# Moving the Gelu loads to ScalarE's queue, cutting the gate loads finer, and one exponential two units later

## What is computed

```
h = x + (sigmoid(ga) * (HGRN2(xn) @ W_a) + sigmoid(gb) * (FoX(xn) @ W_b)) @ W_out
h = h + PEER(RMSNorm(h))
return RMSNorm(h)

# PEER: 8 heads, 128 x 128 keys, 16384 experts, u_table and v_table of 16384 rows x 1024
s1, i1 = top_k(s[:, :, 0], 16);  s2, i2 = top_k(s[:, :, 1], 16)
top_s, pos = top_k(all 256 sums of a pair, 16);  idx = i1*128 + i2 at pos
gates = softmax(top_s)                      # 8 x 16 experts for a token
y = sum over those 128 experts of gate * gelu(u_table[idx] . x) * v_table[idx]
```

## Time and profile before

| | |
|---|---|
| median of 3 runs | 1632.82 us (1631.94 to 1637.9) |
| the profiled execution, its own time | 1630.5 us |
| its span | 1628.7 us |
| TensorE, busy share of the span | 98% |
| VectorE, ScalarE, GpSimd | 78%, 45%, 57% |
| memory traffic | 457.80 MB, mean 281 GB/s |

### The profile page before, as it was taken

How to read it: one execution, slowest core, us unless ns; L and a number is a source line. 1 busy time by engine, 2 the same in 40 slices (tenths; PEclk the granted TensorE clock), 3 DMA queues, 4 the chain that set the end, 5 groups by cost and what they waited for, 6 DMA issues and landing times.

```text
span 1628.7 us, 25977 instructions
## 1 busy us (share of the span) xinstructions
PE 1590.7 (98%) x9763; PEld 1481.1 (91%) x9763; DVE 1270.4 (78%) x2389; ACT 739.9 (45%) x1278; POOL 933.2 (57%) x554
## 2 busy tenths in 40 slices
PE   9999999999999999989999999999999999999996
PEld 7788777788888999989999999999999999999996
DVE  7876645654532899999999878748988989889894
ACT  5533335644321434345677788833333333333333
POOL 4545422434442798988766668785556556465540
PEclk9999999999999999999999999999999999999998
DMA  8322423265343899999988889999999999999981
GB/s 232 104 78 53 110 85 91 87 196 174 112 130 105 284 361 347 344 341 336 344 310 331 320 320 413 417 396 399 405 405 404 398 404 404 404 404 398 406 340 52
DMA packets 216165, 457.80 MB, mean 281 GB/s; under 512 B 15136, under 2 KB 106656, under 8 KB 214504
## 3 DMA queue, kind: packets, MB, share of 16 engines
q1 hardware_dynamic: 145304, 221.29, 39.8%
q0 software_dynamic: 46080, 167.79, 26.4%
q10 hardware_dynamic: 24656, 67.05, 10.7%
HBM read 401.59 MB, written 54.46 MB: 280 GB/s over the span
## 4 chain that ended last, share of the span: by engine, by line
PE 30%; DMA 17%; DVE 13%; issue 5%; ACT 1%; POOL 1%; POOLq 0%; DVEq 0%; ACTq 0%; SPq 0%
DMA raw<-in_v_tab 13%; PE bank L294 8%; PE bank L295 7%; PE bank L296 7%; PE bank L2015 4%; DMA rows<-in_u_rows,expert 3%; DVE spl_a L288 2%; DVE rows L1383 2%; DVE hot L1885 1%; ACT spl_a L284 1%; PE x_rows L294 1%; PE x_rows L296 1%; PE x_rows L295 1%; DVE lists L1734 1%; DVE slot L1798 1%
## 5 line engine op out<-in xcount | busy, mean ns | idle before, releaser
L288 POOL TENSOR_TENSOR spl_a<-raw,spl_a 128x1024 fp32r<-128x1024 f32 x166 | 400.8, 2416 | 215.9 <-ACT spl_a L284 213.6
L284 ACT ACTIVATE spl_a<-raw 128x1024 fp32r<-128x1024 f32 x294 | 309.8, 1055 | 420.4 <-PE bank L296 178.2
L1374 POOL DMA_INDIRECT rows<-in_v_tab,expert x160 | 266.5, 1666 | 203.5 <-DVE hot L1885 177.6
L294 PE MATMUL bank<-x_dense,spl_a 128*128 128x352 f32 x1024 | 335.8, 328 | 2.6 <-POOL spl_a L288 1.4
L296 PE MATMUL bank<-x_dense,spl_a 128*128 128x352 f32 x1024 | 328.5, 321 | 0.0
L295 PE MATMUL bank<-x_dense,spl_a 128*128 128x352 f32 x1024 | 328.4, 321 | 0.0
L294 PE MATMUL bank<-aws,spl_a 128*128 128x352 f32 x768 | 248.7, 324 | 13.0 <-DVE aws L1865 12.2
L295 PE MATMUL bank<-aws,spl_a 128*128 128x352 f32 x768 | 247.1, 322 | 0.0
L296 PE MATMUL bank<-aws,spl_a 128*128 128x352 f32 x768 | 247.1, 322 | 0.0
L1383 DVE SCALAR_TENSOR_TENSOR rows<-rows,x_rows 128x1024 f32<-128x1024 f32 x156 | 188.5, 1210 | 37.3 <-DMA rows<-in_u_rows,expert 34.5
L1885 DVE SCALAR_TENSOR_TENSOR hot<-rows,dot_rows,hot 128x1024 f32<-128x1024 f32 x157 | 197.5, 1278 | 1.3 <-DMA rows<-in_v_tab,expert 1.3
(11 more groups left out here) (362 smaller groups left out, 3058.8 us busy)
## 6 DMA issues: line engine op xcount, KB each, us to landing
raw<-in_u_t SPq DMA_DIRECT2D x128, 512.0 KB
raw<-in_v_tab SPq DMA_DIRECT2D x128, 512.0 KB
dense_gates<-mixbuf ACTq DMA_DIRECT2D x11, 2048.0 KB
raw<-in_w_in SPq DMA_DIRECT2D x42, 512.0 KB
gelu_ux<-gl ACTq DMA_DIRECT2D x58, 352.0 KB
mixbuf<-gelu_ux SPq DMA_DIRECT2D x19, 704.0 KB, 14.1
late_gates<-dense_gates ACTq DMA_DIRECT2D x12, 768.0 KB
raw<-in_w_q SPq DMA_DIRECT2D x16, 512.0 KB
```

What stands on the lines that cost most here:

```text
L284: eng.activation(spl(n, 0, slice(0, W)), raw[:, s, :], ACT.Copy).then_inc(hi_done, 1)
L288: eng.tensor_tensor(spl(n, 1, slice(0, W)), raw[:, n % RAW, :], spl(n, 0, slice(0, W)).bitcast(F32), ALU.subtract) \
L294: nc.tensor.matmul(out, w_hi, x_hi, start=first, stop=False)
L1374: pool.indirect_dma_start(out=rows[:, g % ROWS, :], out_offset=None, in_=u_rows[:, :] if g < STEPS else v_rows, in_offset=bass.IndirectOff ...
```

## The change

Three edits. `mix_gelu` is issued by ScalarE, at units 1, 5, 9, ... of its V loop and ahead of that unit's gate load; SyncE's queue keeps the chunks alone. A piece of gates is two batches (512 KB, the sixth 256 KB), and the six pieces of a group are issued at steps 0, 2, 5, 7, 10 and 12 from the group's first unit, so group 1 at units 1, 3, 6, 8, 11 and 13; the counts that `weight` waits for follow. The exponential of the second tile goes from unit 46 to 48 of the first product, and its transposes from unit 48 to 50.

```diff
         def mix_gates(queue, group, piece):
-            batches = slice(3 * piece, min(3 * piece + 3, DT // TB))
+            batches = slice(2 * piece, min(2 * piece + 2, DT // TB))
...
-            EXP_AT = [22, 46, 69, 93]
-            SLOTS_AT = [None, 48, 72, 98]
+            EXP_AT = [22, 48, 69, 93]
+            SLOTS_AT = [None, 50, 72, 98]
...
-                    part_no = (j - NC) // 4 + 3
-                    if j >= NC and j % 4 == 1 and part_no < NC // 4:
-                        sp.wait_ge(a_mult, 2 * (part_no - 3) + 2)
-                        mix_gelu(sp, part_no)
...
+                    part_no = j // 4 + 3
+                    if j % 4 == 1 and part_no < NC // 4:
+                        act_e.wait_ge(a_mult, 2 * (part_no - 3) + 2)
+                        mix_gelu(act_e, part_no)
                     for group in range(1, NC // GROUP):
                         first = GROUP * (group - 1) - 2 if group > 1 else 1
...
-                        if j - first in (0, 3, 6, 9):
-                            mix_gates(act_e, group, (j - first) // 3)
+                        for piece, step in enumerate((0, 2, 5, 7, 10, 12)):
+                            if j == first + step:
+                                mix_gates(act_e, group, piece)
...
-                        dve.wait_ge(gates_mixed[group % 2], 16 + 64 * (group // 2) if group % 2 == 0
-                                    else 64 * (group // 2 + 1))
+                        dve.wait_ge(gates_mixed[group % 2], 16 + 96 * (group // 2) if group % 2 == 0
+                                    else 96 * (group // 2 + 1))
```

## The result

The changed kernel takes 1636.26 us (median of 11 runs, 1635.24 to 1638.51), the kernel before 1634.19 us (11 runs beside them, 1629.85 to 1638.48). The ratio is 1.0021, 95% interval 1.0011 to 1.0031: 3.4 us slower by the ratio, small but clear of noise. The forecast was 1632.4, 0.4 us under the median then known. The time lies inside the range, the direction is wrong. The prediction also held that a measurement of this kernel can't tell less than 0.5%; this one tells a tenth of a per cent. The profiled execution has a span of 1633.3 us where the one before had 1628.7.

The account below looks back on a forecast made before the run. DMA bytes were taken to bound the second product while rows are gathered. Terms -0.5 - 1.0 - 0.9 + 2.0 = -0.4 took the profiled 1630.5 us to 1630.1; the median's 2.3 us more gave 1632.4, range 1622 to 1640.

Parts of the forecast that it names:

- The bound: Second product while rows are gathered: bytes bind, 3.93 us per unit at 403 GB/s against TensorE's 3.78.
- The rival in which the ceiling gives way: Second product: chunks come in time, traffic rises from 403 to 419 GB/s, total 1620 us; chance 0.15.
- Part 2: Gelu loads on ScalarE's queue, second product: gains only by filling traffic dips; -1.0 us, bounds 0 and 2.4.
- Part 3: Six gate pieces over twelve units, second product: -0.9 us, against +2.0 for VectorE's unpaid stop in group 1.
- the 8 us of stop: Group 1, second product: VectorE stands 3 to 12 us for the sixth piece of gates; 8 taken.
- The piece's landing: Group 1's sixth piece of gates, issued at unit 13, lands between 1170 and 1179 us.
- 13 us at 403 GB/s: Four chunk and six row buffers hold 5.2 MB, so DMA keeps working while VectorE stops.
- The rival on the slow side: Group 1's gates come late, VectorE's 12 us stop is unpaid, slow clock behind it; total 1644 us, chance 0.12.
- Part 1: First product, exponential and transposes two units later: 5.11 us idle removed, mostly returning behind unit 54; -0.5 us, bounds 0 and 1.8.
- The finer pieces: Second product: the last group's gates asked for until three units later; -0.9 us, bounds 0 and -0.9.
- The later groups at 0: Groups after the first: last piece issued four units, 15 us, before use, against 8 us to land; no cost.
- ScalarE's issues at 0: Second product: ScalarE issues 29 and 14 more loads at 0.37 us each, 16 us, within its waits; no cost.

Follow-up runs that it names:

- group 1 at once: Changed kernel with group 1's six pieces of gates issued two at a time at units 1, 2 and 3; ratio 1.0001 to the kernel before.
- Gelu loads alone: Kernel before with only the Gelu loads moved to ScalarE's queue, four pieces of gates as before; ratio 1.0013.
- the exponential alone: Kernel before with only the exponential at unit 48 and its transposes at unit 50; ratio 0.9993 (0.9984 to 1.0002).
- group 1 early: Changed kernel with group 1's six pieces of gates at units 1, 2, 4, 5, 7 and 8; ratio 0.9981 to the kernel before.

## Why the prediction was wrong

**The bound** was right. Second product: 403 GB/s before, 404 and 405 in undisturbed windows after, and 18 us gained when 10 MB are left out. The rival in which the ceiling gives way didn't happen: no slice of the second product passed 406. The 435 GB/s of the Trainium skill (DMA: Bandwidth & Descriptors, "Where 436 GB/s comes from"), by which DMA wouldn't have bound there, is its ceiling for the ports; the same section has about 358 GB/s bind for loads from HBM. This case fits neither: the level is 404, no slice of any run is above 418, and the measurement decides.

**Part 2, the queue.** That the wait would only change its owner was right: table chunks 85.1 us to 1.0, rows 1.3 to 22.5. The dips were filled as forecast: from 1200 to 1500 us no window of 4 us of the changed kernel is under 385 GB/s, where the kernel before has 350, 380 and 332, and the traffic is 405 instead of 402 to 404. What this is worth in time no run shows by itself, since the same edit makes the stop; alone the kernel is 2 us slower.

**Part 3, the failed step** is "Unpaid are between 0 and 8 us; nearest to the buffers, I take +2.0", and the 8 us of stop before it. The mechanism was named, with its place. Both sizes were too small: the stop is 12.9 us, past even the upper bound of 12, and 6.1 us of traffic were lost, three times the 2.0. The piece's landing was inside its bounds (1177.6, for 1170 to 1179); it was VectorE that came early, at 1164.7 instead of 1167.26. The buffers' "13 us at 403 GB/s" was wrong in two ways. It counted them as empty when VectorE stops, while chunks were already ahead by then: from 1164 to 1176 SyncE's queue moves 1.13 MB, half of the four chunk buffers, and DMA runs dry ten us in; and it left out the restart, in which traffic stays short after the stop. With 6.1 in place of 2.0 the sum is +3.7, and the ratio says +3.4. That they agree so well is partly luck, since the other three terms weren't measured as the sum has them: part 2 by no run, part 1 and the finer pieces at other sizes, below. The rival on the slow side had the right mechanism and too high a price, 13.4.

**Part 1** has the right mechanism: no wait at the transposes, the idle time at the first block. Its term of -0.5 took the slow clock's cost for fixed, 1.4 us, carried over from the first place. In the profiled execution it was 3.4 us, and TensorE came out 1.0 late, not 0.4 ahead; but other executions of the same first product lost 1.7 us or nothing there, so the 1.0 is no property of the edit. Alone the edit measures -1.1 (-2.6 to +0.3), so this decides nothing.

**The finer pieces**, -0.9 with that as their bound, measure -3.3 alone (-4.7 to -1.8): the direction is right, the size is past the bound, and no run shows where the rest comes from.

**The later groups at 0** and **ScalarE's issues at 0** held in the changed kernel: one stop in seven groups, and issues of loads that take 0.37 us at the median and 1.17 at most. The second would not hold in general, as group 1 at once shows.

**What made it slower** is shown by two runs that differ from the changed kernel in little: earlier steps for one group take 6.5 us off, and Gelu loads back on SyncE's queue with the exponential as before take 6.7 off (1.0021 against 0.998). Together the parts are worse than their sum: 1.0013, 0.998 and 0.9993 would give 0.9986.

What stays open: with a stop of 10.8 us (Gelu loads alone) the second product takes 514.0 us, with 12.9 us 512.9, though 361 GB/s from 1160 to 1200 us are 4.3 us short and 342 are 6.1. Two us of this are its earlier start (1103.5 against 1105.6). The rest no run isolates.

## What to carry to other kernels

In a stage whose bytes are the bound, a stopped engine cost, as near as these runs tell, only what the DMA engines lost: look at GB/s through the stop and behind it before you price the idle time of anything else. Before two kinds of loads share a queue, add up what stands ahead of the one with the nearest deadline, at the first group above all, where there was no time to run ahead. And when a wait is moved off one step, move the step that takes it over as well: here the exponential alone gave nothing that can be told, and with the first three blocks up to two units later as well, 4.6 us.

## What the hardware showed that I had not expected

Issuing is not always cheap. A load issued by ScalarE took 0.37 us with little outstanding, and up to 4.93 us in the kernel with group 1 early:

```profile
1124.39 4.93 ACTq L1351 DMA_DIRECT2D late_gates<-dense_gates  x1
1129.42 1.06 ACT L284 ACTIVATE spl_a<-raw 128x1024 fp32r<-128x1024 f32 x1 [5.02 <-issue]
```

ScalarE computes nothing in that time. What it depends on isn't shown. The long issue is that of the sixth load within 12 us here, but in group 1 at once it is already among the first three, and in the changed kernel four loads from 1115.16 to 1125.22 are issued in 0.37 to 0.51 us each.

A load in such a queue can also land later than its bytes say: 256 KB took 29.36 us from issue to use, with two Gelu parts and five pieces issued ahead of it and two more Gelu parts behind; it was there at 1170.09, and I had expected 1162.5.

The granted clock is not the same from one execution to the next. After nearly the same idle time in the same place (3.1, 3.5 and 3.9 us) nothing, 1.7 and 3.4 us were lost to 1.2 GHz. After the 11.8 us of idle time in the second product the mean was 0.50 and 0.52 in two windows of 4 us; what that cost beside the lack of traffic can't be told.
